# Mixture-of-experts kernel: one-hot TensorE products pick and scatter the expert rows, and light jobs alternate with heavy ones

## The reference

```python
# DEPTH 2, SEQ 256, D_MODEL 1024, D_FF 3584, N_EXPERTS 8, TOP_K 2, float32
for layer in range(DEPTH):
    h = rms_norm(x, norm_mix[layer])
    x = x + token_mixer(h, ...)                      # four gated branches
    h, m = rms_norm(x, norm_cross[layer]), rms_norm(mem, norm_mem[layer])
    x = x + memory_cross_attention(h, m, ...)
    h = rms_norm(x, norm_ffn[layer])
    x = x + (swiglu(h, ...) if layer % 2 == 0 else moe_ffn(h, ...))
return rms_norm(x, norm_final)

def moe_ffn(h, router_w, w_gu, w_down):
    logits = (h @ router_w).astype(jnp.float32)
    top_val, top_idx = lax.top_k(logits, TOP_K)
    top_w = jax.nn.softmax(top_val, axis=-1)
    gate = jnp.sum(jax.nn.one_hot(top_idx, N_EXPERTS) * top_w[..., None], axis=-2)
    out = jnp.zeros_like(h)
    for e in range(N_EXPERTS):
        out = out + gate[..., e:e + 1] * swiglu(h, w_gu[e], w_down[e])
    return out
```

## Time and profile before

| | |
|---|---|
| median of 3 runs | 1890.59 us (1890.07 to 1890.64) |
| profiled execution | 1890.2 us |
| span of its trace | 1888.4 us |
| TensorE busy | 1821.7 us (96%) |
| DMA read from HBM | 531.11 MB |
| granted TensorE clock, mean | 0.999 of 2.4 GHz |

### The profile page before, as it was taken

The page is one execution under the profiler, slowest core; times in us unless marked ns, Lnnn a source line. Parts: engine busy times, 40 slices in busy tenths (PEclk is TensorE's granted clock), DMA queues, the critical chain, the costliest instruction groups (busy, mean ns, idle before and its releaser), DMA issues.

```text
span 1888.4 us, 30487 instructions
## 1 busy us (share of the span) xinstructions
PE 1821.7 (96%) x13168; PEld 1097.2 (58%) x13168; DVE 794.1 (42%) x1098; ACT 571.6 (30%) x766; POOL 103.0 (5%) x188
## 2 busy tenths in 40 slices
PE   8999999999999999999999999999999999997756
PEld 7887888888888888788885333333333333332111
DVE  7877767655555677776755110101001010101013
ACT  6566555544343446664542000000000000000001
POOL 5300000000000030001000010000000000000010
PEclk9999999999999999999999999999999999999999
DMA  8445655455555554557558999999999999999996
GB/s 303 155 140 174 156 186 185 143 178 185 194 180 196 171 171 142 174 159 242 198 216 318 366 419 418 420 419 420 419 419 418 419 417 414 420 415 421 420 417 268
DMA packets 157256, 542.57 MB, mean 287 GB/s; under 512 B 11416, under 2 KB 35552, under 8 KB 128448
## 3 DMA queue, kind: packets, MB, share of 16 engines
q1 hardware_dynamic: 153120, 529.39, 74.6%
q0 software_dynamic: 3472, 10.91, 1.5%
q10 hardware_dynamic: 528, 0.29, 0.1%
HBM read 531.11 MB, written 9.45 MB: 286 GB/s over the span
## 4 chain that ended last, share of the span: by engine, by line
PE 86%; SPq 7%; DMA 4%; DVE 1%; ACT 1%; issue 1%; POOL 0%; DVEq 0%; ACTq 0%
PE bank L2764 24%; PE bank L2306 13%; PE bank L2308 13%; PE bank L2307 13%; PE bank L2778 8%; SPq L691 4%; PE bank L2792 4%; PE bank L2698 3%; DMA ring<-in_moe_w_down 3%; PE bank L2354 2%; PE bank L2696 2%; SPq L689 1%; SPq L673 1%; PE bank L2372 1%; PE bank L2394 1%
## 5 line engine op out<-in xcount | busy, mean ns | idle before, releaser
L2764 PE MATMUL bank<-ring,o_buf 128*32 128x512 f32 (+1 forms) x5632 | 539.6, 540 | 30.4 <-DMA ring<-in_moe_w_gu 30.4
L2306 PE MATMUL bank<-w_hi,stat 128*128 128x512 f32 (+1 forms) x1168 | 458.0, 392 | 0.3 <-DVE low_in_place L2241 0.3
L2308 PE MATMUL bank<-w_hi,stat 128*128 128x512 f32 (+1 forms) x1168 | 452.9, 388 | 0.0
L2307 PE MATMUL bank<-low_in_place,stat 128*128 128x512 f32 (+1 forms) x1168 | 452.8, 388 | 0.0
L1411 DVE TENSOR_TENSOR low_in_place<-raw,w_hi 128x2048 fp32r<-128x2048 f32 (+1 forms) x161 | 367.7, 2285 | 136.9 <-ACT w_hi L937 136.0
L2764 PEld LDWEIGHTS bank<-ring,o_buf 128*32 128x32 f32 x5632 | 178.7, 110 | 390.4 <-issue 332.0
L937 ACT ACTIVATE w_hi<-raw 128x2048 fp32r<-128x2048 f32 (+1 forms) x161 | 305.8, 1904 | 224.5 <-DMA raw<-in_dense_w_gu 60.9
L2306 PEld LDWEIGHTS bank<-w_hi,stat 128*128 128x128 f32 x1168 | 219.6, 188 | 50.0 <-issue 5.9
L2308 PEld LDWEIGHTS bank<-w_hi,stat 128*128 128x128 f32 x1168 | 219.5, 188 | 44.9
L2307 PEld LDWEIGHTS bank<-low_in_place,stat 128*128 128x128 f32 x1168 | 219.8, 188 | 42.7
L1974 DVE TENSOR_TENSOR area<-bank,area 128x512 f32<-128x512 f32 (+1 forms) x48 | 30.3, 685 | 491.9 <-PE bank L2764 491.9
(11 more groups left out here) (370 smaller groups left out, 1201.0 us busy)
## 6 DMA issues: line engine op xcount, KB each, us to landing
ring<-in_moe_w_gu SPq DMA_DIRECT2D x128, 1024.0 KB, 15.9
ring<-in_moe_w_gu SPq DMA_DIRECT2D x128, 768.0 KB, 16.0
ring<-in_moe_w_down SPq DMA_DIRECT2D x64, 1024.0 KB, 15.8
raw<-in_w_in SPq DMA_DIRECT2D x55, 1024.0 KB, 5.0
ring<-in_moe_w_down SPq DMA_DIRECT2D x32, 1536.0 KB, 16.0
raw<-in_dense_w_gu SPq DMA_DIRECT2D x28, 1024.0 KB, 5.1
raw<-in_w_xkv SPq DMA_DIRECT2D x16, 1024.0 KB, 5.3
raw<-in_dense_w_down SPq DMA_DIRECT2D x14, 1024.0 KB, 5.0
```

Source lines behind the costliest of these rows:

```text
L2306: pe.matmul(dst, x_hi, wh, start=start, stop=False)
L2307: pe.matmul(dst, x_hi, wl, start=False, stop=False)
L2308: return pe.matmul(dst, x_lo, wh, start=False, stop=stop)
L2764: ins = pe.matmul(dsts[g][rows_of(j), 0:n], x_t[:, g, k, :], w[:, j, :, :], start=(k == 0), stop=(k == KD - 1))
```

## The change

- The last four ranks are light jobs. `JOB_ORDER` runs the ranks as 0, 4, 1, 5, 2, 6, 3, 7: heavy and light in turns, the last one light.
- Nothing goes through DRAM but the inputs and the output. `h_rows`, `table_rows`, `last_rows_of`, `y_rows` and all DMAs on them are gone, with the zero rows stored at 882 us.
- After the second tile step of D0 of each job, TensorE picks the rows of the next job with one-hot products (`rows_of_next`): 24 products of 256 columns in the four strips if the next job is heavy, 16 if it is light; then four 128 x 128 transposes of the weighted one-hot matrix. ScalarE copies both out of PSUM; VectorE transposes and scales the rows as before.
- After step 1 of each job TensorE scatters the job before (`scatter_job`): eight products of 512 columns for a heavy one, four for a light one, and VectorE adds the four banks to `x` (`scattered`).
- VectorE builds the one-hot matrices of a job (`picks`), and GpSimd only copies its slot numbers (`slots_of_job`).

```diff
-ROUTE_IDS = 5
-LIGHT = 2
+ROUTE_IDS = 6
+LIGHT = 4
+JOB_ORDER = (0, 4, 1, 5, 2, 6, 3, 7)
+SCATTER_AT = 1
...
             for n in range(LAYER_BLOCKS, LAYER_BLOCKS + MIX_BLOCKS):
                 load_planned(n)
 
-            def store_y(j):
-
-                sp.wait_ge(y_copied_act, j)
-                sp.wait_ge(y_copied_dve, j)
-                for h in range(2):
-                    rows = y_rows[bass.ds(j, 1), :, h * 512:(h + 1) * 512].rearrange("z (b a i) c -> a i (z b) c", a=2, i=GROUP)
-                    for a in range(2):
-                        sp.dma_start(rows[a], y_sb[rows_of(2 * h + a), :, :]).then_inc(y_stored, 16)
-
...
-                if o == STORE_AT:
-                    sp.wait_ge(tokens_act, 2)
-                    sp.dma_start(h_rows.rearrange("(t p) d -> p t d", p=P), quartered).then_inc(rows_stored, 16)
-            sp.wait_ge(zeros_stored, 16 * len(NEVER_STORED))
             sp.wait_ge(routed, 1)
             for j in range(1, E):
-                e = sp.value_load(route_i[0:1, j:j + 1], min_val=0, max_val=E - 1)
+                rank = JOB_ORDER[j]
+                e = sp.value_load(route_i[0:1, rank:rank + 1], min_val=0, max_val=E - 1)
                 for o in range(len(JOB)):
                     load_expert(e, o, j)
-                    if o == STORE_AT:
-                        store_y(j)
...
-            gp.memset(got, 0.0).then_inc(zeros_made, 1)
-            gp.wait_ge(zeros_made, 1)
-            for j in NEVER_STORED:
-                gp.dma_start(y_rows[j, :, :], got).then_inc(zeros_stored, 16)
...
-            gp.wait_ge(lasts_ready, 1)
-            for i, ap in enumerate((last_at, last_gate)):
-                gp.dma_start(last_rows_of[i, :].rearrange("(t p) -> p t", p=P), ap, allow_slow_non_contiguous=True).then_inc(lasts_stored, 16)
-            gp.wait_ge(lasts_stored, 16 * 2)
-            gp.dma_start(last_spread, last_rows_of.rearrange("(a i) n -> a i n", a=1).broadcast_to([P, 2, T])).then_inc(lasts_landed, 16)
-            gp.wait_ge(table_copied, 1)
-            gp.dma_start(table_rows, table).then_inc(table_stored, 16)
-            gp.wait_ge(table_stored, 16)
-            for q in range(STRIPS):
-                gp.dma_start(quarter_tables[rows_of(q), :, :],
-                             table_rows[0:CAP, :].rearrange("(g n) j -> n g j", n=GROUP)).then_inc(table_landed, 16)
-            gp.wait_ge(rows_stored, 16)
-            gp.wait_ge(zeros_stored, 16 * len(NEVER_STORED))
-            gp.wait_ge(tables_read, 1)
+            gp.wait_ge(tables_ready, 1)
+            for n in range(2):
...
+
+            def slots_of_job(j):
+                gp.tensor_copy(slot_now[:, :, :, :], job_slots[:, :, :, bass.ds(j, 2)]).then_inc(slots_chosen, 1)
+
+            slots_of_job(0)
             gp.wait_ge(routed, 1)
             n_jobs = gp.value_load(route_i[0:1, N_MORE:N_MORE + 1], min_val=0, max_val=ROUTE_IDS) + E
...
-                gp.wait_ge(x_gathered, j)
-                gp.tensor_copy(token_now[:, :], slot_token[:, :, bass.ds(j, 1)].rearrange("p g j -> p (g j)")).then_inc(token_chosen, 1)
-                gp.wait_ge(token_chosen, j)
-                gp.nop(nofuse=True)
-                for g in range(GROUPS_X):
-                    gp.indirect_dma_start(got[:, g * 256:(g + 1) * 256], None, h_rows.rearrange("t (q d) -> (t q) d", q=STRIPS),
-                                          bass.IndirectOffsetOnAxis(ap=token_now[:, g:g + 1].bitcast(U32), axis=0)).then_inc(got_landed, 16)
-
-            gp.wait_ge(y_stored, (n_jobs - 1) * (16 * STRIPS))
-            gp.wait_ge(x_gathered, n_jobs)
-            gp.nop(nofuse=True)
-            for k in range(4 * NT):
-                gp.indirect_dma_start(back[k], None, y_rows.rearrange("j p d -> (j p) d"),
-                                      bass.IndirectOffsetOnAxis(ap=token_row[:, k:k + 1].bitcast(U32), axis=0)
-                                      ).then_inc(back_landed, 16)
+                gp.wait_ge(picks_made, j)
+                slots_of_job(j)
 
...
                     act.activation(rrt[:, 0, 0:1], eps_sb[:, :], ACT.Sqrt)
+                act.wait_ge(rows_full, j + 1)
+                if not last:
+                    act.activation(got[:, 0:512], gate_banks[0][:, :], ACT.Copy)
+                    act.activation(got[:, 512:768], gate_banks[1][:, 0:256], ACT.Copy).then_inc(rows_copied, 1)
+                act.wait_ge(pick_turned, j + 1)
+                act.activation(turned_pick, gate_banks[2][:, :].rearrange("p (b t) -> p b t", b=2), ACT.Copy).then_inc(pick_copied, 1)
                 act.wait_ge(expert_used, expert_done(j, len(JOB) - 1))
-                if not first:
-                    act.wait_ge(y_stored, j * (16 * STRIPS))
                 act.activation(y_sb[:, 0, :], bank[6][:, :], ACT.Copy).then_inc(y_copied_act, 1)
...
-            def back_rows():
-
-                dve.wait_ge(back_landed, 16 * 4 * NT)
-                for k in range(4 * NT):
-                    t, c = k // 4, k // 2 % 2
-                    if k % 4:
-                        dve.wait_ge(back_added, k)
-                    dve.scalar_tensor_tensor(out=x[:, t, :], in0=back[k], scalar=rt_gate[:, t, c:c + 1], in1=x[:, t, :],
-                                             op0=ALU.mult, op1=ALU.add).then_inc(back_added, 1)
+            def picks(j):
+
+                dve.wait_ge(slots_chosen, j + 1)
+                if isinstance(j, int):
+                    dve.wait_ge(consts_ready, 6)
+                for t in range(NT):
+                    dve.tensor_scalar(pick[:, t, :], slots_iota[:, 0:CAP], slot_now[:, 0, t, 1:2], None, ALU.is_equal)
+                    ins = dve.tensor_scalar(gate_pick[:, t, :], pair_slots, slot_now[:, 0, t, 0:1], slot_now[:, 1, t, 0:1],
+                                            ALU.is_equal, ALU.mult)
+                ins.then_inc(picks_made, 1)
+
+            def scattered(j):
+
+                for i in range(2 * NT):
+                    t, half = i // 2, i % 2
...
             def expert_job(j, first, last=False):
 
+                if not first:
+                    scattered(j - 1)
                 expert_hidden(j, 0, first)
                 expert_turned(j, 0)
-                if first:
-                    tables_taken()
+                picks(j)
                 expert_hidden(j, 1, first)
                 expert_turned(j, 1)
-                if last:
-                    back_rows()
-                else:
+                if not last:
                     gathered(j + 1)
                 dve.wait_ge(expert_used, expert_done(j, len(JOB) - 1))
-                if not first:
-                    dve.wait_ge(y_stored, j * (16 * STRIPS))
                 dve.tensor_copy(y_sb[:, 1, :], bank[7][:, :]).then_inc(y_copied_dve, 1)
 
-            def scattered(t, half):
-
-                dve.wait_ge(scatter_full, 2 * t + half + 1)
...
+                    pe.wait_ge(pick_copied, j)
+                elif o == U0 and not first:
+                    pe.wait_ge(scatter_added, j * (2 * NT))
...
-            def expert_job(j, first, groups=GROUPS_X):
+            def rows_of_next(j, groups):
+
+                if isinstance(j, int) and j == 0:
+                    pe.wait_ge(tokens_act, 2)
+                pe.wait_ge(picks_made, j + 1)
+                pe.wait_ge(ffn_silu.sem, ffn_silu.at(j, "1"))
+                for g in range(groups):
+                    for t in range(NT):
+                        for q in range(STRIPS):
+                            ins = pe.matmul(gate_banks[g // 2][rows_of(q), g % 2 * 256:g % 2 * 256 + 256], pick[:, t, rows_of(g)],
+                                            quartered[:, t, q * 256:(q + 1) * 256], start=(t == 0), stop=(t == NT - 1))
+                ins.then_inc(rows_full, 1)
+                for b in range(2):
+                    for t in range(NT):
+                        at = (2 * b + t) * P
+                        ins = pe.transpose(gate_banks[2][:, at:at + P], gate_pick[:, t, b * P:(b + 1) * P], ident[:, :])
+                ins.then_inc(pick_turned, 1)
+
+            def scatter(t, full, groups):
+
+                for b in range(groups - 1):
+                    for h in range(2):
+                        rows = slice(64 * h, 64 * h + 64)
+                        ins = pe.matmul(scatter_bank(t, h)[:, :], turned_pick[rows, b, t * P:(t + 1) * P], y_sb[rows, b, :],
+                                        start=(b == 0), stop=(b == groups - 2))
+                        if b == groups - 2:
+                            ins.then_inc(full, 1)
+
+            def scatter_job(j, full, groups):
+
+                pe.wait_ge(y_copied_act, j + 1)
+                pe.wait_ge(y_copied_dve, j + 1)
+                pe.wait_ge(pick_copied, j + 1)
+                for t in range(NT):
+                    scatter(t, full, groups)
+
+            def expert_job(j, first, groups=GROUPS_X, groups_before=GROUPS_X, groups_next=GROUPS_X):
 
                 for o in range(len(JOB)):
```

(48 more changed lines are left out.)

144 lines of the change are left out of this document (35 added, 109 removed).

## The result

| | before | after |
|---|---|---|
| median | 1890.33 us (4 runs) | 1859.10 us (4 runs, 1858.78 to 1859.23) |
| span of the profiled execution | 1888.4 us | 1857.3 us |
| last down products start | 1872.95 us | 1843.32 us |
| HBM read and written | 531.11 + 9.45 MB | 523.88 + 1.05 MB |

The ratio is 0.9835, with a 95% interval of 0.9819 to 0.9850: 31 us or 1.65% faster. The forecast was 1859.

A forecast was written before the change was run, and what follows sets the result against it. Heavy jobs were taken as TensorE's, light ones as the DMA's, DMA full in both. 1872.95 - 23.6 (bytes) - 7.2 (lead) + 1.4 (job 0) = 1843.5, plus 14.05 tail = 1857.6 span, 1859.8 median; stated 1859 us, range 1850 to 1870.

The forecast's parts named there:

- Two bounds, one full stream: Expert jobs: TensorE bounds heavy jobs by some 3 us, the DMA light ones; the DMA engines are full in both.
- Bytes: Job 0's end to the last weight: 9.8 MB less traffic at 416 GB/s moves the end 23.6 us earlier.
- Lead: At job 0's end, 2.5 MB of loads in flight instead of 5.5 MB: gain 3.0 MB, 7.2 us.
- Job 0's end: Job 0 stays TensorE's and, with 2.7 us for picking and transposes, ends at 1128.3 instead of 1126.9 us.
- TensorE keeps up: Each heavy and light pair needs 192.2 us of TensorE against 210.8 us of DMA, so 18 us are spare.
- Handshakes: Waits between engines at each job's start and around picking and scattering cost nothing, covered by down products and steps 2 to 7.
- Loads that wait for space: SP's weight loads: none waits for ring space except in job 0; the ring of 14.68 MB holds 3.1 MB behind.
- Draining between tile shapes: Four insertions a pair, picking and scattering, might each cost one more us for emptying the array; same end either way.
- A: Rival: weights go no faster than heavy jobs' 407 GB/s, so removed traffic frees nothing; time 1876 us; 6%.
- B: Rival: TensorE becomes the bound, a pair takes 215 us; time 1893 us, no change; decides from 18 us more per pair; 2%.
- C: Rival: the fifth expert exceeds 64 tokens and spills into another heavy job, 105 us of weights; time 1966 us; 4%.
- D: Rival: TensorE's clock falls from 2.4 to 1.2 GHz in the four light jobs; time above 2000 us; 1%.

## Why the prediction was right

- **Two bounds, one full stream.** Shown by the kernel before with four light jobs and with turns: both 1890, with waits in the place of work. One reading of the prediction was too strong: the heavy jobs were not TensorE's by some 3 us. With the rows' traffic the DMA was full in them too (418 GB/s), and two heavy jobs made light gained nothing. The sum didn't use this, as it counts the DMA's bytes.
- **Bytes.** 9.8 MB at 416 GB/s, 23.6 us. The DMA view lost 12.4 MB between the two ends; 9.8 are the traffic, the other 2.6 weights that had landed by the end of job 0. 7.34 MB of traffic put back cost 17.2 us for a forecast 17.6.
- **Lead.** Forecast 7.2 us, from 5.5 to 2.5 MB in flight. The books after: 297.95 MB less 0.93 of instructions and some 0.5 of final gain leaves 296.5, against 293.6 for a full ring: 2.9 MB in flight, so 2.6 MB and 6.2 us gained. Putting job 0's traffic back cost 6.1 us by the medians and 5.2 by the traces. The size is right within 1 to 2 us; of the way to it one thing was off, as the two causes don't add but share job 0's room.
- **Job 0's end.** 1128.3 forecast, 1127.56 measured. Its chain begins at:

```profile
1016.76 72.30 PE bank L2669 x768
```

  So job 0 took 110.80 us where it had taken 109.48, 1.3 us more for a forecast 1.4. It also started 0.66 us earlier than in the trace before, which is a difference between runs: in the twelve traces of this case the start lies from 1016.58 to 1017.79. Of the parts, the transposes took 0.59 us, not 1.0: the eight records of the earlier trace rows are eight transposes, which I took for four, so that group's title and the term are off by a factor of two.
- **TensorE keeps up.** 192.2 us a pair forecast, 191.9 measured; the DMA's 210.8 was 211.9. Job 2 shows no wait for weights, and from job 3 on each light job does. I had light jobs waiting from job 3; job 1 already waited three times at its end, 2.6 us in all.
- **Handshakes at nothing.** The waits of PE in the kernel after from job 0's end to the last product have two rows, both for weights:

```profile
PE bank L2683 <- DMA ring<-in_moe_w_down: 22.4, 26, 1.9
PE bank L2669 <- DMA ring<-in_moe_w_gu: 22.1, 52, 1.0
```

  Nothing waits for ScalarE, VectorE or GpSimd.
- **Loads that wait for space.** The prediction said that none would after job 0, and that is wrong. The waits of SP in the kernel after from 1210 to 1843 us come to 138 us in 73 times; the largest row:

```profile
SPq L671 <- PE bank L2697: 94.6, 36, 4.7
```

  The DMA stands at 420 GB/s all the same, because the loads already in the queue keep it full: 26.8 us at 416 GB/s are 11 of the ring's 14.7 MB. A wait of the issuing engine for space is thus no sign of a DMA that runs dry.
- **Draining between tile shapes** (the Trainium skill, TensorEngine Tiling (Array Packing), Key Properties: a change of tiling mode drains the engine). The chain has 3.63 us for the eight products of a heavy scattering and 1.92 us for the four of a light one. So a product takes 0.43 us, and 0.21 us are left that don't scale. This agrees with a small price for the change of mode, but that the 0.21 us are the drain is not shown. They are a fifth of the 1 us that I had set as the bound. Four of them in a pair are under 1 us, and the pair came out at its sum anyway.
- **Tail.** 14.0 us against 14.05. The additions start at 1848.09, 4.8 us after the last product's start, where it was 5.7.
- **The sum.** 1843.5 forecast and 1843.32 measured for the last product. This closeness is partly luck, since parts that were off cancelled: the lead gave 1.0 us less than forecast, job 0 ended 0.8 us earlier (0.66 of it by its start), and the rate was 416.3 instead of 416.0 GB/s, worth 0.4 us. The full sum gave 1859.8 us, of which I stated 1859; that the median is 1859.10 and not 1859.8 is luck too.

The rivals: weights at 407 GB/s (A) fell with 420 in the first full pair. TensorE as the bound (B) came only with 30 us more per pair, where 18 were forecast as its point: with 13 more it is still hidden. A ninth job (C) and a slower clock (D) didn't come; the granted clock stood at 1.00 in every window above, and in each of the four light jobs alone.

## What to carry to other kernels

When two resources are both nearly full, take the stream apart by bytes: a part of the DMA's traffic that looks like 3% is worth its full time as soon as nothing else holds the end. Moving that traffic to an engine helps only if this engine has slack near by; slack that comes only after the heavy work does nothing for it (four heavy jobs first held the DMA at 384 GB/s for 345 us), so let heavy and light work alternate within the buffer's depth, here 3.1 MB behind in a heavy job against a ring of 14.7. And price neither half of such a change alone: here one alone cost 15 us, the other gave none, and both gave 31.

## What the runs showed of the hardware that I had not expected

512 stores of 4 bytes each, 2 KB in all, took some 2 MB of throughput from a stream at 375 GB/s for 10 us (the earlier trace rows and the kernel with these stores put back).

Scattering products of 64 x 128 tiles between strips of 128 x 32 cost 0.2 us for each insertion beyond their own time (3.63 and 1.92 us for eight and four products).

TensorE's busy time overstates its work where it waits often: 197.5 us a pair by the windows, 191.9 us by the kernel that picks eight times.
